# Splitting fp32 weights into high and low parts in pieces of 1024 instead of 512 columns per partition

## What is computed

```python
xn = rmsnorm(x, g_mix)
z = xn @ w_in                                    # 1024 -> 3584
a, u, v, ga, gb = jnp.split(z, ...)
pa, new_hist = pool_mixer(a, hist, pos0, w_pool, pool_scale)
pb, vn = gmlp_mixer(u, v, g_v, w_spatial, b_spatial)
merged = jax.nn.sigmoid(ga) * (pa @ w_up_pool) + jax.nn.sigmoid(gb) * (pb @ w_up_gmlp)
h = x + merged @ w_out
hn = rmsnorm(h, g_ffn)
# top-1 group of 4, then top-2 of its 4 experts; expert e on its rows xb:
hid = jax.nn.silu(xb @ w_gate[e]) * (xb @ w_up[e])   # 1024 -> 512
y = hid @ w_down[e]                                  # 512 -> 1024
```

## Time and profile before

| | |
|---|---|
| median of 3 runs | 2008.78 us (2006.15 to 2011.86) |
| the profiled execution, its own time | 2014.13 us |
| its span, first to last instruction | 2012.4 us |
| mean granted TensorE clock | 0.958 |
| PE busy | 1877.3 us (93%) |
| PEld busy | 1609.9 us (80%) |
| DVE busy | 974.0 us (48%) |
| ACT busy | 773.4 us (38%) |
| POOL busy | 280.8 us (14%) |
| DVE subtractions of 512 columns for panels, and for gate and up | 352 of 686 ns; 256 of 688 ns mean |
| ACT copies of 512 columns for panels, and for gate and up | 352 of 619 ns; 240 of 617 ns |

### The profile page before, as it was taken

How to read it: one execution, slowest core, us unless ns; L and a number is a source line. 1 busy time by engine, 2 the same in 40 slices (tenths; PEclk the granted TensorE clock), 3 DMA queues, 4 the chain that set the end, 5 groups by cost and what they waited for, 6 DMA issues and landing times. The chain is left out here.

```text
span 2012.4 us, 28492 instructions
## 1 busy us (share of the span) xinstructions
PE 1877.3 (93%) x10232; PEld 1609.9 (80%) x10233; DVE 974.0 (48%) x1929; ACT 773.4 (38%) x1442; POOL 280.8 (14%) x387
## 2 busy tenths in 40 slices
PE   7899999999999999999999937999999999999980
PEld 5899987788888788887888736888888888888870
DVE  5634343546444654445454334445565554646424
ACT  4332323333333333333333204444465444636423
POOL 2000000000201001000010022222222222222223
PEclk9799999999999999999999958999999999999995
DMA  6222233423236222342232517655567566556438
GB/s 220 88 83 84 84 128 119 138 86 102 85 126 209 84 85 96 135 138 93 84 105 87 198 47 230 186 183 184 177 215 257 152 230 188 183 182 228 130 56 343
DMA packets 153429, 293.12 MB, mean 146 GB/s; under 512 B 9341, under 2 KB 75901, under 8 KB 153354
## 3 DMA queue, kind: packets, MB, share of 16 engines
q1 hardware_dynamic: 135930, 232.13, 32.9%
q0 software_dynamic: 15072, 51.45, 10.4%
q10 hardware_dynamic: 2352, 8.52, 1.0%
HBM read 243.02 MB, written 49.07 MB: 145 GB/s over the span
## 5 line engine op out<-in xcount | busy, mean ns | idle before, releaser
L62 PE MATMUL bank<-xT_hi,wh 128*128 128x512 f32 (+1 forms) x960 | 341.0, 355 | 7.2 <-ACT S L745 5.4
L63 PE MATMUL bank<-xT_lo,wh 128*128 128x512 f32 (+1 forms) x960 | 340.4, 355 | 0.0
L64 PE MATMUL bank<-xT_hi,wl 128*128 128x512 f32 (+1 forms) x960 | 339.2, 353 | 0.0
L793 DVE TENSOR_TENSOR wl<-raw,wh 128x512 fp32r<-128x512 f32 x352 | 219.4, 686 | 202.5 <-ACT wh L596 202.4
L1665 PE MATMUL bank<-gu_hi,ex_hi 128*128 128x256 f32 (+1 forms) x960 | 311.6, 325 | 4.6 <-DVE gu_lo L1575 4.6
L1667 PE MATMUL bank<-gu_hi,ex_lo 128*128 128x256 f32 (+1 forms) x960 | 307.3, 320 | 0.0
L1666 PE MATMUL bank<-gu_lo,ex_hi 128*128 128x256 f32 (+1 forms) x960 | 307.3, 320 | 0.0
L596 ACT ACTIVATE wh<-raw 128x512 fp32r<-128x512 f32 x352 | 192.0, 619 | 85.1 <-PE bank L1216 54.7
L62 PEld LDWEIGHTS bank<-xT_hi,wh 128*128 128x128 f32 x960 | 182.3, 190 | 35.9 <-issue 9.7
L1665 PEld LDWEIGHTS bank<-gu_hi,ex_hi 128*128 128x128 f32 x960 | 183.5, 191 | 24.7 <-DVE gu_lo L1575 8.2
L64 PEld LDWEIGHTS bank<-xT_hi,wl 128*128 128x128 f32 x960 | 182.4, 190 | 25.3
(11 more groups left out here) (228 smaller groups left out, 3154.8 us busy)
## 6 DMA issues: line engine op xcount, KB each, us to landing
raw<-in_w_in SPq DMA_DIRECT2D x56, 1024.0 KB, 5.2
raw_gate_up<-in_w_gate SPq DMA_DIRECT2D x16, 2048.0 KB, 8.4
raw_gate_up<-in_w_up SPq DMA_DIRECT2D x16, 2048.0 KB, 13.5
raw_d<-in_w_down SPq DMA_DIRECT2D x16, 2048.0 KB, 12.8
raw<-in_w_out SPq DMA_DIRECT2D x16, 1024.0 KB, 6.3
raw<-in_w_up_pool SPq DMA_DIRECT2D x16, 512.0 KB, 3.5
raw<-in_w_up_gmlp SPq DMA_DIRECT2D x16, 512.0 KB, 4.5
h<-in_x_prompt SPq DMA_DIRECT2D x16, 512.0 KB, 5.0
```

Of the source, the lines that this page charges most:

```text
L62: nc.tensor.matmul(out, lh, rh, start=(i == 0), stop=False)
L63: nc.tensor.matmul(out, lh, rl, start=False, stop=False)
L64: last = nc.tensor.matmul(out, ll, rh, start=False, stop=(i == n - 1))
L793: lo = lambda out, x, hi: tt(out, x, hi.bitcast(F32), ALU.subtract)
```

## The change

A piece is now two slices, 1024 columns. A panel is split in two pieces in place of four. Gate and up of an expert are 8 pieces in place of 16: DVE copies slices 0 and 1 itself and subtracts both in one instruction, ACT makes the other 7 pieces (and `weigh` stands before the last of them, at the same slice as before), and TensorE waits for piece k // 2 ahead of slice k. The counts of the semaphores follow. The down weights, which were split in 1024 columns already, stay as they are. No load, matmul or buffer is added, taken away or moved.

```diff
-SPLITS = 20
+PIECES = KD
+SPLITS = PIECES + KH
 SPLITS_ACT = SPLITS - 1
...
         def part(w, q):
-            return w[:, 2 * q:2 * q + 2, :]
+            return w[:, 4 * q:4 * q + 4, :]
...
# ACT, split of a panel
-                for q in range(4):
+                for q in range(2):
                     nc.scalar.activation(part(wh[par], q), part(raw[par], q), ACT.Copy).then_inc(w_hi, 1)
...
# DVE, split of a panel
-                for q in range(4):
-                    dve.wait_ge(w_hi, 4 * n + q + 1)
+                for q in range(2):
+                    dve.wait_ge(w_hi, 2 * n + q + 1)
                     last = lo(part(wl[par], q), part(raw[par], q), part(wh[par], q))
...
# SP, load(e)
-                    sp.wait_ge(e_lo, SPLITS * e + (KD - SPLITS))
+                    sp.wait_ge(e_lo, SPLITS * e + (PIECES // 2 - SPLITS))
...
-                    sp.wait_ge(e_lo, SPLITS * e + (2 * KD - SPLITS))
+                    sp.wait_ge(e_lo, SPLITS * e + (PIECES - SPLITS))
...
# ACT, split of an expert
-                    for k in range(1, 2 * KD):
-                        if k == KD:
+                    for q in range(1, PIECES):
+                        if q == PIECES // 2:
                             act.wait_ge(up_in, 16 * e + 16)
-                        if k == KD + 6:
+                        if q == PIECES - 1:
                             weigh(lo)
-                        nc.scalar.activation(gu[0][:, k, :], raw_gu[:, k, :], ACT.Copy).then_inc(e_hi, 1)
+                        nc.scalar.activation(gu[0][:, 2 * q:2 * q + 2, :], raw_gu[:, 2 * q:2 * q + 2, :], ACT.Copy)\
+                            .then_inc(e_hi, 1)
...
# DVE, split of an expert
-                    copy(gu[0][:, 0, :], raw_gu[:, 0, :])
+                    copy(gu[0][:, 0:2, :], raw_gu[:, 0:2, :])
                     dve.drain()
-                    for k in range(2 * KD):
-                        if k:
-                            dve.wait_ge(e_hi, SPLITS_ACT * e + k)
-                        lo_half(gu[1][:, k, :], raw_gu[:, k, :], gu[0][:, k, :]).then_inc(e_lo, 1)
+                    for q in range(PIECES):
+                        ks = slice(2 * q, 2 * q + 2)
+                        if q:
+                            dve.wait_ge(e_hi, SPLITS_ACT * e + q)
+                        lo_half(gu[1][:, ks, :], raw_gu[:, ks, :], gu[0][:, ks, :]).then_inc(e_lo, 1)
...
# TensorE, per_block
-                        pe.wait_ge(e_lo, SPLITS * e + k + 1)
+                        pe.wait_ge(e_lo, SPLITS * e + k // 2 + 1)
...
-                        pe.wait_ge(e_lo, SPLITS * e + KD + k + 1)
+                        pe.wait_ge(e_lo, SPLITS * e + (KD + k) // 2 + 1)
```

More of the change, by code:

```diff
@@ L1625, in down @@
                         if first:
-                            dve.wait_ge(e_hi, SPLITS_ACT * e + 2 * KD + k)
+                            dve.wait_ge(e_hi, SPLITS_ACT * e + PIECES + k)
                             lo_half(dn[1][:, k, :], raw_d[:, k, :], dn[0][:, k, :]).then_inc(e_lo, 1)
@@ L1702, in per_block @@
                     for k in range(KH):
-                        pe.wait_ge(e_lo, SPLITS * e + 2 * KD + k + 1)
+                        pe.wait_ge(e_lo, SPLITS * e + PIECES + k + 1)
                         if k == 2:
```

## The result

| | before | after |
|---|---|---|
| median of 6 runs each | 2007.94 us (2006.15 to 2011.86) | 2022.02 us (2020.06 to 2025.96) |
| ratio, 95% interval | | 1.0069 [1.0055, 1.0083] |
| the profiled execution, its own time; span | 2014.13; 2012.4 us | 2022.04; 2020.4 us |
| mean granted clock | 0.958 | 0.960 |
| PE, DVE, ACT busy | 1877.3, 974.0, 773.4 us | 1878.8, 957.7, 738.6 us |

DVE and ACT each run 304 instructions fewer and work 16 and 35 us less, and the kernel takes 14 us longer. The forecast was 2021.1 (2014.5 to 2026.0), slower.

The account below looks back on a forecast made before the run. The prediction took TensorE, never idle in the expert stage, to bound the kernel. 12.8 us at the expert heads less 0.5 in the prompt stage gave 12.3, taking the median from 2008.78 to 2021.1 us (range 2014.5 to 2026).

Parts of the forecast that it names:

- What bounds the kernel: Expert stage: TensorE is busy for 671.00 of 671.00 us, so anything added to its waits is added to the time.
- The forecast's signs: Expected in the changed profile: TensorE idle 0.7 to 0.8 us per head, 15 PEld waits for `gu_lo` of about 1.0.
- Copy +0.267, subtraction +0.534: At each expert's head, the wider first piece comes later by these two amounts in us, together 0.801 (0.534 to 0.962).
- The start of DVE's copy is not set by anything that the change touches: At an expert's head, DVE's 1.80 us of idle time before the copy is put down to issue, not a wait.
- the term of 12.8 us: Expert heads: TensorE pays 0.801 us once per expert, 16 x 0.801 = 12.8 us (8.5 to 15.4).
- Later pieces: Expert stage: pieces after the first don't stall TensorE; DVE makes one every 1.14 us, TensorE needs 1.38 per pair.
- The end of the split: Each expert: ends 9.97 us after its start, not 10.36; counted at nothing, as DVE waits 0.73 us for TensorE.
- Prompt stage, -0.5 with 1 to either side: Shorter ACT splits save 3 x 0.17 = 0.5 us at three group borders; later pooling behind DVE's split may eat it.
- DVE's total, "46 us less": DVE's total over the whole kernel should fall by (176 + 128) x 0.15 = 46 us, none of it in the time.
- The paced end: Rival, chance 0.04: the end of each expert's split paces TensorE, not its head; 6.7 us less, 2002.1.
- The swallowed delay: Rival, chance 0.08: the `dn_lo` wait in each first block, 5.3 us in all, absorbs the head delay; 2011.5.
- The falling clock: Rival, chance 0.04: idle time at expert heads lowers the granted clock, 16 x 1.6 = 25 us on top; 2046.

Follow-up runs that it names:

- run 304: Not a run label: in this sentence "run" is a verb; in the changed kernel DVE and ACT each execute 304 instructions fewer than in the kernel before.
- the high part first: Changed kernel, but for each pair of gate slices TensorE runs the four matmuls needing only the high part first: 2007.94 us, ratio 0.9990 to the kernel before.
- the wide copy alone: Against the changed kernel, DVE's copy stays 1024 wide but slices 0 and 1 are subtracted one by one in 512: 2017.56 us, ratio 1.0028 to the kernel before.
- The dose of 2048 columns: Changed kernel with each expert's first piece 2048 columns wide, the other six pieces 1024: 2066.65 us, ratio 1.0274 to the kernel before.
- experts alone: Changed kernel with the prompt stage back at 512 columns, experts split in 1024: 2022.84 us, ratio 1.0057 to the kernel before.
- with the head healed: Changed kernel with slices 0 and 1 of each expert as 512-column pieces, the other 14 slices in seven of 1024: 2022.08 us, ratio 1.0042 to the kernel before.
- The prompt stage alone: Kernel before with only the prompt stage split in 1024 columns, experts still in 512: 2009.85 us, ratio 0.9996 to the kernel before.
- late-end run: Changed kernel with each expert's last gate and up subtraction done twice and counted after the second: 2022.32 us, ratio 1.0057 to the kernel before.
- shifted twin: Kernel before with eight small memsets on DVE ahead of the loop over the experts: 2009.29 us in one run.

## Why the prediction was right, and where it was off

- **What bounds the kernel: right.** TensorE had no idle time between 1228 and 1899 us, and has 6.65 us now. All of it lies at the heads, about 0.48 at each, and the order of six matmuls takes it away (666.00 of 666.00 with the high part first). The forecast's signs were a little too large: 0.7 to 0.8 us of idle time at a head (the records of matmuls overlap), and waits of PEld of about 1.0 us, where they took 0.89.
- **Copy +0.267, subtraction +0.534: right.** From copy to first low part it went from 1.20 to 1.99 us, +0.79. The two terms apart: +0.26 with the wide copy alone. The dose of 2048 columns followed the same line, 3.60.
- **"The start of DVE's copy is not set by anything that the change touches": wrong by 0.13 us.** The idle time ahead of it went from 1.78 to 1.65, and a head cost 0.70 rather than 0.80. With the idle time at 1.78 (experts alone) it cost 0.80 without the first head. So the term of 12.8 us was 16 x 0.695 = 11.1.
- **Later pieces: right for this change.** The prediction compared rates, 1.14 us a piece against 1.38. That is enough where TensorE has waited for a first piece as wide as the others: no later piece stalled. It doesn't carry over to narrow pieces ahead of wide ones, where it also counts how far DVE is ahead when the first wide piece begins: with the head healed, the third piece stalled instead (0.60 us).
- **The end of the split: right.** DVE waits 1.97 us there for TensorE, and 1.3 us more of work were swallowed.
- **Prompt stage, -0.5 with 1 to either side: not contradicted, but the gain was eaten.** The prompt stage alone measured -0.8 [-2.6, +1.0]. At the second and third border TensorE's wait went from 1.58 and 1.59 to 1.40 us, the 0.17 that was counted; at the first from 1.96 to 1.39, since 0.45 us of idle time of DVE, put down to issue, was gone as well ahead of the pooling step (L915) that ACT follows. That is 0.94 us back. But the prediction feared that the later pooling "may eat the 0.5", and it ate more: behind each border TensorE now waits 0.42 to 0.45 us for `pa_lo`, 1.31 us that the kernel before doesn't have. The kernel with the prompt stage alone shows these three waits too, and the one with the experts alone doesn't. The two kinds of panels can't be told apart in the start of the first expert's copy: 1217.61 to 1220.72 us in three profiles with 512, 1216.84 to 1222.88 in nine with 1024, means 1218.7 and 1218.9.
- **DVE's total, "46 us less": wrong, it was 16.3.** The step took 0.15 us a pair from the durations of single instructions, 2 x 688 against 1222 ns. But successive ones overlap in time: 16 take 9.86 us, 4 take 2.50. From those rows it is 88 x (2.50 - 2.36) + 16 x 0.39 = 18.6. The time doesn't hang on it.
- **Rivals.** The paced end falls with the late-end run. The swallowed delay falls with `dn_lo` at 5.3 us as before. The falling clock doesn't happen at 0.49 us of idle time at a head, and mostly does at 2.08.

The sum was 12.3 us; the medians differ by 14.1, and the interval of the ratio allows 11.0 to 16.7. The traces account for 11.1 at the heads, and for the other 3 us no trace shows a place; runs of one kernel scatter by as much either way. That the median came within 1 us of 2021.1 is therefore in part luck: the term of the heads was 1.7 us too high, and what is not accounted for made up for it.

The rule that the prediction cites from the Trainium skill (Perfetto Trace Analysis, section Optimizing Scalar/DVE Operations) is borne out in its sign: the engines were not saturated, and longer instructions made a bubble on TensorE, 10.4 us over 15 heads. But breaking the instructions up again is not the only way out; TensorE can also do first what needs the early half.

## What to carry to other kernels

Ask of a wider producer piece how late its *first* result comes, and how far the producer is ahead at that point: with 0.08 us of lead gained per slice, the first piece of double width stalled TensorE at slice 0 and at slice 2, and no longer at slice 8. Then ask whether the consumer can begin with what is finished first: here it began with the high part after 0.69 us, not the low part after 1.99, and the width of the pieces stopped mattering. Before paying for fewer instructions, look whether the engines that save them are waited for anywhere else; here 16 us less on DVE and 35 on ACT were worth nothing by themselves.

## What was unexpected of the hardware

- The 1.65 to 1.86 us of idle time on DVE at the start of each expert, put down to issue, takes one of three values (1.65, 1.78, 1.86), the same at all heads of a kernel but the first within 0.05 us, and changes with code outside the loop in a way that a shift of eight instructions doesn't reproduce. It was worth 0.08 us a head between 1.78 and 1.86 (prompt stage only against before) and 0.11 between 1.65 and 1.78 (experts only against the changed kernel).
- With 2.05 to 2.09 us of idle time at each head the granted clock fell to 0.50 behind 13 of the 15 heads after the first, and not behind the other two; each fall cost 1.6 us. At 0.49 us it never fell, nor behind the 1.96 us at the first border of the prompt stage.
- Falls of the same size come and go in the prompt stage between executions. One row each, of the kernel before and of its shifted twin, whose prompt stage is the same program. Both begin 0.6 us ahead of the same matmul, before which TensorE was idle for 0.40 us behind short router products and transposes:

```profile
909.00:914.00 5.00, 4.60 (x15) 3.55 (x13) 3.85 (x6) 3.78 (x8) 0.27 (x1) 0.66 0.17 53
```

```profile
907.12:912.12 5.00, 4.60 (x22) 3.61 (x20) 3.85 (x6) 3.79 (x8) 0.27 (x1) 1.00 0.16 51
```

So the idle time alone doesn't tell whether the clock falls. Such falls are part of the scatter of some 3 us either way that runs of one kernel show.
